# Four low parts of the last token quarter on GpSimd instead of VectorE, and their high parts earlier on ScalarE

## The chip, the cores and the metric

The program runs on one core of a Trainium2 chip. The metric is the device time in microseconds (us) of one execution; the median of three runs of the kernel before is 2413.59 us (2409.25 to 2414.49).

## The reference

A backbone of two layers on 1024 latent tokens and 256 context tokens, width 1024. Layer 0: a combined projection, neighbourhood attention and a bidirectional recurrence, an output projection. Layer 1: a gated short convolution. Each layer ends in a SwiGLU feed-forward block of hidden width 2816. What the change touches is the first projection of three blocks:

```
h = h + g2 * swiglu(modulate(rmsnorm(h, norm2_g[l]), sh2, sc2), w_gu, w_down)   # layer 0 and layer 1
bg, cg, xv = split(modulate(rmsnorm(h, norm1_g), sh1, sc1) @ w_in, 3)           # short convolution
```

All arithmetic is float32. Every output of these blocks is a product of the modulated tokens with a 1024-row weight matrix.

## The kernel before, in words

**Split operands.** A float32 operand is written as a high part (rounded by a copy, on ScalarE) and a low part (full minus high). A product is three matmuls per 128 rows of the contraction: L1014 (high weights, high tokens), L1015 (low weights, high tokens) and L1016 (high weights, low tokens).

**Stages.** Three stages use one scheme: F0 (feed-forward of layer 0), S (short convolution) and F1 (feed-forward of layer 1). Each has a joint (normalise the tokens, make the operands), then "pairs" of output tiles (22, 12 and 22), then the down projection. A pair of tiles is computed by a seven-product scheme on halves of the contraction and halves of the tokens: the products 0 to 6 take sums and differences of token quarters and of weight quarters, and VectorE adds the seven results in PSUM. Products 0 and 3 of the first four pairs are done ahead, in the joint, from their own slots. Product 6 takes the token quarter `a22`, which needs no sum. Products 1, 2, 4 and 5 take sums that VectorE makes: sums 1 and 2 go to `low_f`, their high and low parts to `act_lo`; sums 4 and 5 are made in `x_rms`, with high and low parts in `act_hi`. Each operand consists of four blocks of 128x512, k = 0 to 3.

**Order of the joint (all queues are written by hand, each engine runs its own in order).**

- ScalarE (`joint`, L1524): modulates the second half of the tokens, then `token_high` (L1470) for 1, 2, then `operand_high` (L1491, a high part of the weights, tile `slot_hi`) for product 4, `token_high` for 5, `operand_high` for 5, `token_high` for 4, `operand_high` for 6, `token_high` for 6.
- VectorE (`joint`, L1944): `token_sum` 1 and 2, `token_low` 1 (L1937), `token_sum` 5 (L1929) in turns with `token_low` 2, `token_sum` 4 (L1931) in turns with `token_low` 4, `token_low` 5, `pair_first` (L2012, L2014: the first two PSUM additions of pair 0), `token_low` 6. Then `pair_work` of pair 0 (L2027 `t_pad`, the weight sums L1901 and L1906 for pair 1, L2032, L2034 `t_pad`, L1909, and so on).
- GpSimd: the low parts of the weights, `operand_low` (L975, tile `slot_lo`), for products 1, 2, 4, 5, 6 of pair 0, then pair after pair.
- TensorE (`pair_products`, L1331): products 1, 2, 4, 5, 6. Product n waits for its `slot_lo`; in pair 0 each of its four blocks also waits for its token low part (`ready`). Product 1 of the next pair waits for the PSUM sum C22 (L2034), product 6 for U2 (L2014).
- SyncE: `load_pair` (L683) loads two tiles `raw` of weights for the next pair. They wait for `slot_lo` of product 5 and of product 6 of the pair before; the weight sum L1901 of the next pair waits for both tiles.

Of the kernel before, what the change touches and what calls it, by code (L numbers as in the profile page):

```python
# [24 lines left out]
ALU = mybir.AluOpType  # L25
# [33 lines left out]
def backbone(nc, t):  # L59
# [18 lines left out]
    with es:  # L78
        def sem(name):
            return es.enter_context(nc.semaphore(name))  # L80
# [198 lines left out]
        s_down = {"a0": sem("set_a_first_half_landed"), "a1": sem("set_a_second_half_landed"), "b": sem("set_b_landed"), "c": sem("set_c_landed")}  # L279
        s_h2, s_l2 = sem("down_operand_hi"), sem("down_operand_lo")  # L280
        s_n0, s_fs, s_hs, s_ld = sem("first_half_lo"), sem("token_sums_made"), sem("token_operand_hi"), sem("token_operand_lo")
        s_grow = sem("gain_row_landed")
        s_fturn, s_fsq, s_fstd = sem("fin_turned"), sem("fin_squared"), sem("fin_rms_ready")
        s_fta, s_fpart = sem("fin_first_half_turned"), sem("fin_first_half_squared")
# [76 lines left out]
        REST = (1, 2, 4, 5, 6)  # L361
# [109 lines left out]
            return 16 * st + {1: 2 * k + 1, 2: 2 * k + 2, 5: 8 + k + 1, 4: 12 + k + 1}[n]  # L471

        def highs(st, n, k):
            return 20 * st + 4 * (1, 2, 5, 4, 6).index(n) + k + 1

        def weights_in(st):
            return t["o_w_in"][0] if st == S else t["ffn_w_gu"][0 if st == F0 else 1]
# [323 lines left out]
        def _(pool):  # L801
# [190 lines left out]
            for st in (F0, S, F1):  # L992
                if st != F0:
                    first_lows(st)
                for f in range(FT):
                    first_half_low(st, f)
                if st == F0:
                    first_lows(st)
                operand_low(st, *FIRST[7])
                for n in REST:  # L1000
                    operand_low(st, n, 0)
                for p in range(1, PAIRS[st]):
                    for n in operands(st, p):
                        operand_low(st, n, p)
                for r in range(ROUND[st]):
                    down_low(st, r)
# [3 lines left out]
        def _(pe):  # L1010
# [320 lines left out]
            def pair_products(st, p):  # L1331
                g = PAIR0[st] + p
                every = p >= EARLY
                def ready(n):
                    return (lambda k: (s_ld, 20 * st + 4 * REST.index(n) + k + 1)) if p == 0 else None

                if every:
                    pe.wait_ge(s_xfree, g)
                    operand_product(st, 0, p, x_bank(p))
                if g:  # L1340
                    pe.wait_ge(*made(g - 1, C22))
                operand_product(st, 1, p, P5_BANK, ready(1))
                if g:
                    pe.wait_ge(*made(g - 1, C21))
                operand_product(st, 2, p, P6_BANK, ready(2))
                if every:
                    pe.wait_ge(s_p1, g + 1)
                    operand_product(st, 3, p, x_bank(p))
                operand_product(st, 4, p, P7_BANK, ready(4))
                operand_product(st, 5, p, P3_BANK, ready(5))  # L1350
                pe.wait_ge(*made(g, U2))
                operand_product(st, 6, p, P4_BANK, ready(6))
# [83 lines left out]
        def _(act):  # L1436
# [28 lines left out]
            def token_high(st, n, k):  # L1465
                if n == 6:
                    act.wait_ge(s_nhi, 8 * (NORM[st] + 1) + 2 * k + 2)
                else:
                    act.wait_ge(s_fs, summed(st, n, k))
                nc.scalar.copy(ACTS[n][k][HI], LOW_F[n][k]).then_inc(s_hs, 1)  # L1470
# [53 lines left out]
            def joint(st):  # L1524

                n, n0 = NORM[st], LAST_OUT[st]
                if st != F0:
                    for e in range(7):
                        operand_high(st, *FIRST[e])
                for f in range(FT):  # L1530
                    square(n, f, (s_hup, n0 + f + 3))
                rms(n)
                square(n + 1, 0, (s_hup, n0 + FT + 3))
                if st == S:
                    act.wait_ge(s_const, 5)
                for f in range(FT):
                    first_half(st, f)
                    if f % 2:
                        square(n + 1, 1 + f // 2, (s_hup, n0 + FT + 1 + f // 2 + 3))
                if st == F0:  # L1540
                    for e in range(7):
                        operand_high(st, *FIRST[e])
                for f in range(5, FT):
                    square(n + 1, f, (s_hup, n0 + FT + f + 3))
                first_product_copied(st, 0)
                rms(n + 1)
                first_product_copied(st, 1)
                operand_high(st, *FIRST[7])
                operand_high(st, 1, 0)
                second_half(st, 0)  # L1550
                second_half(st, 1)
                token_high(st, 1, 0)
                operand_high(st, 2, 0)
                second_half(st, 2)
                token_high(st, 1, 1)
                first_product_copied(st, 2)
                second_half(st, 3)
                token_high(st, 1, 2)
                token_high(st, 1, 3)
                for k in range(4):  # L1560
                    token_high(st, 2, k)
                    if k == 1:
                        first_product_copied(st, 3)
                operand_high(st, 4, 0)
                for k in range(4):
                    token_high(st, 5, k)
                operand_high(st, 5, 0)
                for k in range(4):
                    token_high(st, 4, k)
                operand_high(st, 6, 0)  # L1570
                for k in range(4):
                    token_high(st, 6, k)

            def pair_work(st, p):
                ahead = p + 1 if p + 1 < PAIRS[st] else None
# [250 lines left out]
        def _(dve):  # L1826
# [117 lines left out]
            def joint(st):  # L1944

                n, n0, gate = NORM[st], LAST_OUT[st], (G1, G2, MODS + G1)[st]
                for f in range(FT):
                    if st == F0 and f in (0, 3, 6):
                        dve.wait_ge(s_reload[f // 3], 16)
                    update(n0, f, gate, last_bank(st, f))  # L1950
                    if st == S:
                        mods_here(ROUND[F0] - 2, f)
                    if f:
                        add_squares(n, f - 1)
                add_squares(n, FT - 1)
                update(n0, FT, gate, last_bank(st, FT))
                if st == S:
                    mods_here(ROUND[F0] - 2, FT)
                    dve.wait_ge(s_mset, LT + MODS)
                    set_gains((3, mods, MODS + SC1, PAR["n1"] + FT), (4, mods, MODS + SC2, PAR["n2"] + FT))  # L1960
                    dve.wait_ge(s_const, 5)
                inverse_rms(n)
                update(n0, FT + 1, gate, last_bank(st, FT + 1))
                scale(n, 0, 0)
                scale(n, 1, 1)
                add_squares(n + 1, 0)
                for f in range(2, FT):
                    if f < 5:
                        update(n0, FT + f, gate, last_bank(st, FT + f))
                        scale(n, 2 * f - 2, 2 * f - 2)  # L1970
                        scale(n, 2 * f - 1, 2 * f - 1)
                    else:
                        update(n0, FT + f, gate, last_bank(st, FT + f))
                    add_squares(n + 1, f - 1)
                add_squares(n + 1, FT - 1)
                weight_sum(st, 1, 0)
                weight_sum(st, 2, 0)
                inverse_rms(n + 1)
                weight_sum(st, 4, 0)
                weight_sum(st, 6, 0)  # L1980
                order = [(i, i // 2 + 4 * (i % 2)) for i in range(8)]
                scale(n + 1, *order[0])
                scale(n + 1, *order[1])
                for k in range(4):
                    if k < 3:
                        scale(n + 1, *order[2 * k + 2])
                    token_sum(st, 1, k)
                    if k < 3:
                        scale(n + 1, *order[2 * k + 3])
                    token_sum(st, 2, k)  # L1990
                for k in range(4):
                    token_low(st, 1, k)
                for k in range(4):
                    token_sum(st, 5, k)
                    token_low(st, 2, k)
                token_sum(st, 4, 0)
                for k in range(4):
                    if k < 3:
                        token_sum(st, 4, k + 1)
                    token_low(st, 4, k)  # L2000
                for k in range(4):
                    token_low(st, 5, k)
                pair_first(st, 0)
                for k in range(4):
                    token_low(st, 6, k)

            def pair_first(st, p):
                g = PAIR0[st] + p
# [359 lines left out]
```

## Time and profile before

| what | us |
|---|---|
| median of three runs | 2413.59 |
| the profiled execution's own time | 2408.06 |
| its span | 2406.2 |
| TensorE matmul busy | 2310.3 (96% of the span) |
| VectorE busy | 1489.1 (62%) |
| GpSimd busy | 1218.6 (51%) |
| ScalarE busy | 844.3 (35%) |

In a timeline each row gives the start, the time taken, the engine, the line, the operation, the tiles (output, arrow, inputs) and a count of merged neighbours; brackets give the idle time of the engine before it and what ended that. The joint of F0 lies at 600 to 667 us of the span, that of S at 1340 to 1407, that of F1 at 1686 to 1753.

### The profile page before, as it was taken

What the parts mean: (1) busy time and instruction counts of PE and PEld (TensorE: products, weight loads), DVE (VectorE), ACT (ScalarE), POOL (GpSimd) and SP (SyncE); (2) the same over time, 40 slices, a digit from 0 to 9 for tenths busy, and PEclk for the clock granted to TensorE, in tenths of its full rate; (3) what the DMA queues carried; (4) which work ended last, traced back from release to release, by engine and by line L of the source; (5) the groups of instructions that cost most, each with busy time, mean ns of one, the idle gap of its engine ahead of it and who ended that gap; (6) DMA issues with size and microseconds to landing.
All of it is one profiled execution on the core that took longest, in us unless ns stands there. A gap on an engine that the chain in (4) does not pass through costs nothing.

```text
span 2406.2 us, 27721 instructions
## 1 busy us (share of the span) xinstructions
PE 2310.3 (96%) x10486; PEld 1866.6 (78%) x10486; DVE 1489.1 (62%) x1951; ACT 844.3 (35%) x1367; POOL 1218.6 (51%) x739
## 2 busy tenths in 40 slices
PE   8999999989999999999898988999999999999998
PEld 3888878878778888877777867887778888888887
DVE  5677748853775455546666797664875445555553
ACT  4544428862532232331111522222632232232122
POOL 3333346888655555564334255555355555565440
PEclk9999999999999999999998999999999999999999
DMA  9444467534123222255454012243023222243222
GB/s 311 157 137 139 156 158 149 97 98 128 48 84 100 80 79 79 79 184 188 157 187 163 23 58 69 77 140 108 14 92 93 87 79 79 79 149 105 92 84 79
DMA packets 265448, 268.65 MB, mean 112 GB/s; under 512 B 43527, under 2 KB 209123, under 8 KB 264803
## 3 DMA queue, kind: packets, MB, share of 16 engines
q1 hardware_dynamic: 258835, 247.99, 33.6%
q10 hardware_dynamic: 5904, 16.78, 2.0%
q8 instruction: 84, 1.38, 0.2%
q0 software_dynamic: 576, 2.10, 0.2%
q14 instruction: 49, 0.40, 0.1%
HBM read 219.28 MB, written 47.55 MB: 111 GB/s over the span
## 4 chain that ended last, share of the span: by engine, by line
PE 78%; DVE 9%; DMA 5%; POOL 3%; ACT 2%; issue 2%; SPq 1%; DVEq 0%; POOLq 0%; ACTq 0%
PE bank L1014 24%; PE bank L1016 24%; PE bank L1015 24%; DMA mod_in_f<-in_mod_w 3%; POOL slot_lo L975 2%; DMA raw<-in_ffn_w_gu 1%; PE bank L1095 1%; DVE probs L2298 1%; PE bank L1225 1%; SPq L740 1%; PE bank L1251 1%; PE bank L1250 1%; DVE act_hi L1937 1%; PE bank L1212 1%; PE bank L1049 1%
## 5 line engine op out<-in xcount | busy, mean ns | idle before, releaser
L975 POOL TENSOR_TENSOR slot_lo<-raw,slot_hi 128x512 fp32r<-128x512 f32 x256 | 414.3, 1643 | 303.1 <-ACT slot_hi L1491 303.1
L1864 DVE SCALAR_TENSOR_TENSOR h<-bank,mods,h 128x512 f32<-128x512 f32 x384 | 284.9, 749 | 268.2 <-PE bank L1016 265.4
L1491 ACT CAST slot_hi<-raw 128x512 fp32r<-128x512 f32 x256 | 153.5, 619 | 361.4 <-DMA raw<-in_ffn_w_gu 234.7
L1014 PE MATMUL bank<-a,slot_hi 128*128 128x512 f32 x672 | 267.1, 398 | 9.8 <-DVE t_pad L2046 6.3
L1016 PE MATMUL bank<-a,slot_hi 128*128 128x512 f32 x672 | 264.6, 394 | 0.0
L1015 PE MATMUL bank<-a,slot_lo 128*128 128x512 f32 x672 | 263.6, 392 | 0.0
L975 POOL TENSOR_TENSOR slot_lo<-t_sum,slot_hi 128x512 fp32r<-128x512 f32 x112 | 168.8, 1528 | 182.2 <-ACT slot_hi L1491 182.2
L2012 DVE TENSOR_TENSOR bank<-bank,p 128x512 f32<-128x512 f32 x56 | 39.0, 697 | 308.5 <-PE bank L1016 308.4
L1014 PE MATMUL bank<-act_lo,slot_hi 128*128 128x512 f32 x448 | 179.6, 401 | 10.0 <-DVE t_pad L2034 8.0
L1014 PE MATMUL bank<-act_hi,slot_hi 128*128 128x512 f32 x448 | 179.1, 400 | 6.8 <-DVE act_hi L1937 6.5
L1016 PE MATMUL bank<-act_hi,slot_hi 128*128 128x512 f32 x448 | 177.7, 397 | 0.0
L1016 PE MATMUL bank<-act_lo,slot_hi 128*128 128x512 f32 x448 | 177.6, 397 | 0.0
L1015 PE MATMUL bank<-act_lo,slot_lo 128*128 128x512 f32 x448 | 177.5, 396 | 0.0
L1015 PE MATMUL bank<-act_hi,slot_lo 128*128 128x512 f32 x448 | 177.3, 396 | 0.0
L1014 PEld LDWEIGHTS bank<-a,slot_hi 128*128 128x128 f32 x672 | 126.6, 188 | 40.9 <-DVE t_pad L2046 6.8
L986 POOL TENSOR_TENSOR act_lo<-low_f,act_lo 128x512 fp32r<-128x512 f32 x80 | 102.0, 1316 | 109.7 <-ACT act_lo L1522 109.7
L1016 PEld LDWEIGHTS bank<-a,slot_hi 128*128 128x128 f32 x672 | 126.6, 188 | 30.4
L1015 PEld LDWEIGHTS bank<-a,slot_lo 128*128 128x128 f32 x672 | 126.8, 189 | 28.8
L1015 PE MATMUL bank<-act_hi,w_lo 128*128 128x512 f32 x376 | 148.0, 394 | 0.0
L1014 PE MATMUL bank<-act_hi,w_hi 128*128 128x512 f32 x368 | 144.8, 393 | 2.7 <-DVE act_lo L2164 2.7
L1491 ACT CAST slot_hi<-t_sum 128x512 fp32r<-128x512 f32 x112 | 69.7, 622 | 219.3 <-DVE t_sum L1901 198.4
L1016 PE MATMUL bank<-act_lo,w_hi 128*128 128x512 f32 x368 | 144.4, 392 | 0.0
(288 smaller groups left out, 5520.8 us busy)
## 6 DMA issues: line engine op xcount, KB each, us to landing
raw<-in_ffn_w_gu SPq DMA_DIRECT2D x88, 512.0 KB, 4.7
mod_in_f<-in_mod_w SPq DMA_DIRECT2D x48, 512.0 KB, 8.3
z_spill<-silu_g SPq DMA_DIRECT2D x88, 256.0 KB, 4.0
mod_in_p<-in_mod_w SPq DMA_DIRECT2D x32, 512.0 KB, 6.5
raw<-in_o_w_in SPq DMA_DIRECT2D x24, 512.0 KB, 4.6
raw<-in_e_w_in SPq DMA_DIRECT2D x20, 512.0 KB, 5.0
low_f<-z_spill SPq DMA_DIRECT2D x40, 256.0 KB, 4.2
a_f<-z_spill SPq DMA_DIRECT2D x18, 512.0 KB, 6.0
```

Of the source, the lines that this page charges most:

```text
L740: sp.dma_start(down_operand(st, r, j, c, h)[2], from_).then_inc(s_down[set_of(st, r) + ("" if h is None else str(h))], 16)
L975: nc.gpsimd.tensor_tensor(slot_lo[:, s, :], from_, slot_hi[:, s, :], ALU.subtract).then_inc(s_wlo, 1)
L986: nc.gpsimd.tensor_tensor(lo, full, hi, ALU.subtract).then_inc(s_l2, 1)
L1014: pe.matmul(dst, w_hi, x_hi, start=first, stop=False)
L1015: pe.matmul(dst, w_lo, x_hi, start=False, stop=False)
L1016: return pe.matmul(dst, w_hi, x_lo, start=False, stop=last)
L1049: mm = pe.matmul(bank[:, b, m:m + 1], acc[:, m * P:(m + 1) * P], ones[:, 0:1], start=True, stop=True)
L1095: mm = pe.matmul(bank[0:2, 4 + 2 * c + a, :], cond[:, k, :], mod_ring[:, u % 8, a * HALF:(a + 1) * HALF], start=(k == 0), stop=(k == FT - 1))
L1212: pe.matmul(out_, q, k_hi[:, hd % 2, src:src + n], start=True, stop=False)
L1491: nc.scalar.copy(slot_hi[:, s, :], from_).then_inc(s_whi, 1)
L1864: V.scalar_tensor_tensor(out=dst, in0=bank[:, b, :], scalar=mods[:, gate, m:m + 1], in1=dst, op0=ALU.mult, op1=ALU.add).then_inc(s_hup, 1)
L2012: V.tensor_tensor(x, x, first, ALU.add).then_inc(s_made, 1)
```

## The change

GpSimd makes the four low parts of product 6's tokens, between `slot_lo` of product 2 and `slot_lo` of product 4. VectorE's four are gone from behind `pair_first`. ScalarE makes the four high parts after those of 2, ahead of `slot_hi` of product 4 and of the high parts of 5 and 4. A new semaphore counts GpSimd's four; the numbering of ScalarE's high parts follows the new order.

```diff
         def highs(st, n, k):
-            return 20 * st + 4 * (1, 2, 5, 4, 6).index(n) + k + 1
+            return 20 * st + 4 * (1, 2, 6, 5, 4).index(n) + k + 1
...
                 operand_low(st, *FIRST[7])
-                for n in REST:
+                operand_low(st, 1, 0)
+                operand_low(st, 2, 0)
+                for k in range(4):
+                    pool.wait_ge(s_hs, highs(st, 6, k))
+                    hi, lo = ACTS[6][k]
+                    nc.gpsimd.tensor_tensor(lo, LOW_F[6][k], hi, ALU.subtract).then_inc(s_lp, 1)
+                for n in (4, 5, 6):
                     operand_low(st, n, 0)
...
                 def ready(n):
-                    return (lambda k: (s_ld, 20 * st + 4 * REST.index(n) + k + 1)) if p == 0 else None
+                    if p:
+                        return None
+                    return lambda k: (s_lp, 4 * st + k + 1) if n == 6 else (s_ld, 16 * st + 4 * REST.index(n) + k + 1)
...
                     if k == 1:
                         first_product_copied(st, 3)
+                for k in range(4):
+                    token_high(st, 6, k)
                 operand_high(st, 4, 0)
...
                 operand_high(st, 6, 0)
-                for k in range(4):
-                    token_high(st, 6, k)
...
                 pair_first(st, 0)
-                for k in range(4):
-                    token_low(st, 6, k)
```

## Rows read from the trace of the kernel before

**Rows 1.** The page, shares of the engines and the chain that ended last.

```profile
PE 2310.3 (96%) x10486; PEld 1866.6 (78%) x10486; DVE 1489.1 (62%) x1951; ACT 844.3 (35%) x1367; POOL 1218.6 (51%) x739
...
PE 78%; DVE 9%; DMA 5%; POOL 3%; ACT 2%; issue 2%; SPq 1%; DVEq 0%; POOLq 0%; ACTq 0%
```

**Rows 2.** TensorE's waits in the whole span: total us, times, longest.

```profile
PE bank L1014 <- DVE t_pad L2034: 8.0, 7, 2.3
...
PE bank L1014 <- DVE a L1937: 1.2, 2, 0.6
```

**Rows 3.** Timeline of TensorE, F0 joint and first pairs, rows with a wait.

```profile
661.88 0.47 PE L1014 MATMUL bank<-a,slot_hi 128*128 128x512 f32 x1 [0.57 <-DVE a L1937]
...
666.94 0.47 PE L1014 MATMUL bank<-act_lo,slot_hi 128*128 128x512 f32 x1 [2.04 <-DVE t_pad L2034]
...
698.02 0.47 PE L1014 MATMUL bank<-act_lo,slot_hi 128*128 128x512 f32 x1 [0.94 <-DVE t_pad L2034]
701.73 0.50 PE L1014 MATMUL bank<-act_lo,slot_hi 128*128 128x512 f32 x1 [0.67 <-DVE p L2052]
714.38 0.50 PE L1014 MATMUL bank<-a,slot_hi 128*128 128x512 f32 x1 [1.18 <-ACT silu_g L1508]
```

**Rows 4.** Timeline of ScalarE, F0 joint.

```profile
643.36 1.14 ACT L1470 CAST act_lo<-low_f 128x512 fp32r<-128x512 f32 x2
644.40 0.62 ACT L1491 CAST slot_hi<-raw 128x512 fp32r<-128x512 f32 x1
...
648.67 0.62 ACT L1470 CAST act_hi<-x_rms 128x512 fp32r<-128x512 f32 x1 [0.58 <-DVE x_rms L1929]
```

**Rows 5.** Timeline of VectorE, F0 joint.

```profile
649.15 1.28 DVE L1931 TENSOR_TENSOR x_rms<-x_rms,a 128x512 f32<-128x512 f32 x2
650.52 1.62 DVE L1937 TENSOR_TENSOR act_hi<-x_rms,act_hi 128x512 fp32r<-128x512 f32 x1
652.07 1.77 DVE L1931 TENSOR_TENSOR x_rms<-x_rms,a 128x512 f32<-128x512 f32 x1
...
661.06 2.48 DVE L1937 TENSOR_TENSOR a<-a_f,a 128x512 fp32r<-128x512 f32 x4
663.47 0.68 DVE L2027 TENSOR_TENSOR t_pad<-bank,p 128x512 f32<-128x512 f32 x1
664.07 0.67 DVE L1901 TENSOR_TENSOR t_sum<-raw 128x512 f32<-128x512 f32 x1
```

**Rows 6.** One line, L975 on GpSimd: count, shortest/median/longest ns, first and last start; the three joints.

```profile
L975 POOL TENSOR_TENSOR slot_lo<-raw,slot_hi x2: 1731/4109/6487, 645.1 to 651.6; 128x512 fp32r<-128x512 f32 x2
...
L975 POOL TENSOR_TENSOR slot_lo<-raw,slot_hi x2: 1725/4107/6489, 1384.6 to 1391.0; 128x512 fp32r<-128x512 f32 x2
...
L975 POOL TENSOR_TENSOR slot_lo<-raw,slot_hi x2: 1732/4117/6502, 1731.5 to 1738.0; 128x512 fp32r<-128x512 f32 x2
```

**Rows 7.** Timeline of GpSimd, F0 joint.

```profile
645.11 8.18 POOL L975 TENSOR_TENSOR slot_lo<-raw,slot_hi 128x512 fp32r<-128x512 f32 x2 [7.74 <-ACT slot_hi L1491]
656.29 1.29 POOL L975 TENSOR_TENSOR slot_lo<-raw,slot_hi 128x512 fp32r<-128x512 f32 x1 [3.00 <-ACT slot_hi L1491]
```

**Rows 8.** Loads of `raw`, 655 to 685 us: landing times, last issue for pair 2, its first use.

```profile
DMA to landing us min/median/max: 3.8/4.0/5.2
...
674.59 0.37 SPq L683 DMA_DIRECT2D raw<-in_ffn_w_gu  x1
...
679.84 0.69 DVE L1901 TENSOR_TENSOR t_sum<-raw 128x512 f32<-128x512 f32 x1 [4.07 <-DMA raw<-in_ffn_w_gu]
```

**Rows 9.** Timelines of VectorE and of TensorE in stage S.

```profile
1403.80 0.68 DVE L1901 TENSOR_TENSOR t_sum<-raw 128x512 f32<-128x512 f32 x1
...
1456.98 0.79 PE L1014 MATMUL bank<-a,slot_hi 128*128 128x512 f32 x1 [6.34 <-DVE t_pad L2046]
```

**Rows 10.** Stretches: us, busy (x count) of PE, PEld, DVE, ACT, POOL, PEclk granted, DMA share, GB/s.

```profile
661.80:664.80 3.00, 2.92 (x12) 2.17 (x12) 2.94 (x5) 0.00 (x0) 0.00 (x0) 1.00 0.00 0
...
1457.00:1462.80 5.80, 5.80 (x14) 4.54 (x15) 5.67 (x5) 0.91 (x2) 4.33 (x3) 0.50 0.31 87
```

More of the change, by code:

```diff
@@ L281, in backbone @@
         s_n0, s_fs, s_hs, s_ld = sem("first_half_lo"), sem("token_sums_made"), sem("token_operand_hi"), sem("token_operand_lo")
+        s_lp = sem("last_token_operand_lo_by_pool")
         s_grow = sem("gain_row_landed")
```

## The prediction

> **What bounds the kernel now.** I read the page's shares first: TensorE is busy 96% and carries 78% of the chain that ended last [rows 1]. Only time in which TensorE stands still, or runs at its lower clock, can be won or lost. The view of waits says who makes it stand: 1.2 us go to the low parts of product 6 (`a`) and 8.0 us to the sum C22 (`t_pad`, L2034), of which F0's joint has 2.04 [rows 2, 3]. The timelines of one joint, F0, give the order; the other two repeat it within a few tenths (their long GpSimd operations last 6489 and 6502 ns against 6487) [rows 6]. I work F0 out in its own times and carry it over.
>
> In F0 product 4 can start at 652.15, when VectorE has its first low part (650.52 + 1.62 = 652.15) [rows 5]. Product 6 starts at 661.88 and product 1 of pair 1 at 666.94 after 2.04 us of idling for C22 [rows 3]. VectorE is behind all three: it works without a pause from 650.52 to C22, and the four low parts to be moved take 661.06 to 663.47, 2.4 us [rows 5].
>
> **What is removed: VectorE.** Taken alone, everything from 663.47 on would come 2.4 us earlier. TensorE could use it: it idles 0.57 + 2.04 = 2.6 us before product 6 and before pair 1 [rows 3]. So the gain on offer is 2.4 us per joint, 7.2 us in all.
>
> **What moves: ScalarE.** The four high parts cost about 0.52 us each (two take 1.14, starts 0.52 apart; 643.36 + 2 x 0.52 = 644.40) and now run from 644.40 to 646.5; `slot_hi` of product 4 ends near 647.1 instead of 645.0 [rows 4]. The high parts of 5 then run behind, but before they had idled 0.58 us for their sum; the fourth still starts at about 648.67 [rows 4]. From there ScalarE is in its old place. Cost 0; if that cover were thin, it is bounded by 2.1 us of work against VectorE's low parts of 5, which come over 6 us later.
>
> **What is added: GpSimd.** Its price is the heart of the matter. `slot_lo` of product 4 is asked for at 645.1, in the middle of a run of VectorE subtractions and additions with both inputs in SBUF, and lasts 6.49 us; alone such an operation takes 1.29 (656.29) [rows 6, 7]. It ends at 651.59, just after VectorE's first pause (649.15 + 1.28 = 650.43 to 650.52). The VectorE operation that starts at 650.52 takes 1.62 us and the next 1.77, where their like take 0.68; GpSimd's second takes 1.73 [rows 5, 6]. So the two don't run side by side: the request that comes into an unbroken run of VectorE waits for a pause (all three joints, [rows 6]), and after that they take turns, GpSimd's ends being 653.29 - 651.59 = 1.70 apart and VectorE losing 1.1 us per turn.
>
> The Trainium skill (SBUF — State Buffer, "Who interferes with whom") says that a VectorE instruction with two SBUF inputs contends with a GpSimd one that reads SBUF, and that whichever issues first gets the shared ports for the whole instruction while the other blocks until it finishes. The trace agrees on the blocking (1.62, 1.77) and not on the wait, which is ten VectorE operations long and not one. By that rule the loss per joint would be 2.3 instead of the 2.9 below.
>
> The first of the four new operations is asked for when ScalarE's first high part of 6 is done, 644.40 + 0.62 = 645.0. That is the same run of VectorE, which the change leaves as it is up to 650.43. So it ends at 651.6, as `slot_lo` of product 4 did, and behind it stand six more in turns of 1.70: the other three end at 653.3, 655.0 and 656.7, `slot_lo` of 4, 5 and 6 at 658.4, 660.1 and 661.8. Before they ended at 651.6, 653.3 and 657.6 [rows 6, 7].
>
> **What is late next.** VectorE waits seven times for about 1.1 us here and had waited three times: low parts of 4 end at 652.15, 655.5, 658.9, 660.6, the first of 5 at 662.3, the last at 664.1 (0.60 apart once GpSimd is through). `pair_first` starts at 664.1 instead of 659.86, its two steps take 1.2, and L2027 starts at 665.3 instead of 663.47: +1.8, although four operations were taken off.
>
> The load of the second `raw` tile for pair 1 is issued at `slot_lo` of product 6, 661.8 instead of 657.6. Loads in this stretch take 3.8 to 5.2 us to land; in pair 2, whose two loads also go out close together, the last is issued at 674.59 and L1901 starts 5.2 us later [rows 8]. Here the two are 1.7 us apart, so I take 5.2: L1901 starts at 667.0 instead of 664.07, +2.9 (with 3.8 it would be +1.5, but then L2027's +1.8 counts). From L1901 to TensorE's restart are 666.94 - 664.07 = 2.9 us as before, hence product 1 of pair 1 at 669.8: **+2.9 us**.
>
> TensorE itself: product 4 waits for `slot_lo` until 658.5, six microseconds of idling that were not there. At the full clock (12 matmuls in 2.8 us, as product 6 of before within its 3.0 us) [rows 10] it ends with its last low part at 661.4, product 5 at 665.2, product 6 at 668.2. After 6.34 us of idling in stage S the granted clock was 0.50, its 1.2 GHz level, for 5.8 us more [rows 9, 10]; with 5.80 / 14 = 0.41 us per matmul for as long, product 6 ends at 669.1. Both are before 669.8, so this stays hidden.
>
> Does the shift last? In pairs 1 to 3 the idling before 698.02 is again for C22, behind an L1901 that waits for its load (4.07 us in pair 2), which waits for `slot_lo` of product 6 [rows 3, 8]. That ring is what got late, so the shift is passed on whole.
>
> In S the same step gives 1401.3 + 5.2 = 1406.5 for L1901, which stood at 1403.8 [rows 9]: +2.6 (its GpSimd operations lie 739.5 us behind those of F0, 1384.6 against 645.1 [rows 6]). F1 is as F0: +2.9. **Sum: 2.9 + 2.6 + 2.9 = 8.4 us.** On the profiled execution's 2408.06 (span 2406.2 plus 1.9 around it) that is 2416.5. This execution lies 5.5 us under the median of the runs shown, so I add the sum to the median: 2413.6 + 8.4 = **2422.0 us**. Bounds from the same rows: +1.8 per joint (5.4, 2419) if the loads come quickly, +4.6 per joint (13.8, 2427.4) in the clock rival below.
>
> **Rivals.**
>
> *Faster: the turns cost VectorE nothing at the wrong place.* If GpSimd's four operations slip in between VectorE's or ScalarE delivers early enough for the 7.74 us in which GpSimd idled before 645.11 [rows 7], the 2.4 us taken off VectorE come through at L2027, product 6 and C22: 3 x 2.4 = 7.2, 2406.4 us. It decides from the point where `slot_lo` of 4 still ends by 653. For it: the real idling behind exactly these operations [rows 2, 3]. Against it: the high parts are ready at 645.0 at the earliest, and three of three requests at this place waited 6.5 us [rows 6]. Chance 0.11.
>
> *No change: the delay is taken up later.* TensorE idles 0.94 + 0.67 + 1.18 = 2.8 us in pairs 3 and 4 of F0 [rows 3] and 6.34 in S [rows 9]. Were these waits for a chain that is not late, 0.1 of F0's 2.9, none of S's 2.6 and, taking F1 as F0, 0.1 there would be left: +0.2, 2413.8 us. Against it stands that the waits end with the same load ring. Chance 0.15.
>
> *GpSimd is let in at once* (the page's order, as a mechanism here: the first new operation runs behind the VectorE operation that is under way at 645.1). Then six turns run from 645.6 to 655.3, the low parts of 2 come out at up to 655.9, those of 4 end near 660.6, `slot_lo` of 6 follows its high part at 662.4, and a lone load (4.0) lets L1901 start at 666.4: +2.3 per joint, 2420.6. VectorE loses the same turns elsewhere. For: the turns of 1.70. Against: rows 6. Chance 0.10.
>
> *The clock decides.* If TensorE stays at 0.50 for some 10 us from 658.5, products 4, 5 and 6 end at 671.5 and not 669.1: +4.6 per joint, 2427.4. For: one stretch of 5.8 us at 0.50 after such an idling [rows 10]; against: it takes nearly twice that in all three. Chance 0.08.
>
> **How the numbers follow.** The forecast, ring and turns with +5.4 to +10 in all, has 0.56. Faster (by over 0.2%, 4.8 us, about what a measurement can tell here) 0.11; within 0.2% 0.15; slower 0.56 + 0.10 + 0.08 = 0.74. The range 2414 to 2428 leaves out the faster case, and a little at the top.
>
> **What would show it.** In each joint: GpSimd's first `a` operation lasts about 6.5 us from 645, then six operations of about 1.73; `slot_lo` of 4 ends near 658.4; TensorE has one idle stretch of about 6 us before product 4; VectorE's operations from 650.5 last 1.7 each, seven in a row; the wait before pair 1 falls from 2.0 to below 1.7, and VectorE's L1901 of pair 1 waits for a DMA. I am wrong if `slot_lo` of 4 ends before 654, or if pair 1 starts less than 1 us later and pairs 3 and 4 show less idling.

## The result and the profile after

The changed kernel takes 2415.4 us (median of 20 runs, 2407.5 to 2423.2), the kernel before in the same jobs 2409.5 us (20 runs, 2403.7 to 2414.5). The ratio is 1.0024 (95% interval 1.0013 to 1.0034): **slower by 5.8 us** (3.1 to 8.2). I had forecast slower by 8.4 us, at 2422.0. The direction came as written, and so did the operations named and their times in F0's joint. The measured size is a third smaller, and the median of three runs on which I put the sum, 2413.6, lies 4.1 us above what 20 runs of the kernel before give.

The profile page of the changed kernel, shares of the engines (compare [rows 1]): GpSimd has the four operations of three joints more, VectorE fewer operations and yet more busy time.

```profile
PE 2313.2 (96%) x10486; PEld 1872.5 (78%) x10486; DVE 1492.2 (62%) x1939; ACT 842.7 (35%) x1367; POOL 1239.3 (51%) x751
```

The view of one line after, the new low parts on GpSimd (L1006) in the joints of F0 and S: count, shortest/median/longest ns, first and last start (compare [rows 6]).

```profile
L1006 POOL TENSOR_TENSOR a<-a_f,a x4: 1710/1714/6508, 644.7 to 654.5; 128x512 fp32r<-128x512 f32 x4
...
L1006 POOL TENSOR_TENSOR a<-a_f,a x4: 1702/1711/6502, 1387.1 to 1396.9; 128x512 fp32r<-128x512 f32 x4
```

The timeline of GpSimd after, F0 joint (compare [rows 7]): four low parts to 656.25, then the weights of 4, 5 and 6 to 661.31.

```profile
644.73 11.52 POOL L1006 TENSOR_TENSOR a<-a_f,a 128x512 fp32r<-128x512 f32 x4 [7.74 <-ACT a L1479]
656.22 5.09 POOL L976 TENSOR_TENSOR slot_lo<-raw,slot_hi 128x512 fp32r<-128x512 f32 x3
```

The timeline of VectorE after, same stretch (compare [rows 5]). The row of 6.94 us stands for six operations, of which the first three last 1.75 to 1.77.

```profile
650.16 1.63 DVE L1946 TENSOR_TENSOR act_hi<-x_rms,act_hi 128x512 fp32r<-128x512 f32 x1
651.72 1.74 DVE L1940 TENSOR_TENSOR x_rms<-x_rms,a 128x512 f32<-128x512 f32 x1
653.38 1.75 DVE L1946 TENSOR_TENSOR act_hi<-x_rms,act_hi 128x512 fp32r<-128x512 f32 x1
655.06 1.74 DVE L1940 TENSOR_TENSOR x_rms<-x_rms,a 128x512 f32<-128x512 f32 x1
656.73 6.94 DVE L1946 TENSOR_TENSOR act_hi<-x_rms,act_hi 128x512 fp32r<-128x512 f32 x6
...
664.90 0.69 DVE L2034 TENSOR_TENSOR t_pad<-bank,p 128x512 f32<-128x512 f32 x1
666.42 0.69 DVE L1910 TENSOR_TENSOR t_sum<-raw 128x512 f32<-128x512 f32 x1 [0.83 <-DMA raw<-in_ffn_w_gu]
...
669.15 0.68 DVE L1918 TENSOR_TENSOR raw<-raw 128x512 f32<-128x512 f32 x1
```

TensorE after, rows of the timeline with a wait (compare [rows 3]), then two stretches (columns as in [rows 10]). One idling of 6.19 us ahead of product 4 takes the place of the small ones; behind it the granted clock is 0.50 for 5.7 us.

```profile
657.98 0.79 PE L1021 MATMUL bank<-act_hi,slot_hi 128*128 128x512 f32 x1 [6.19 <-POOL slot_lo L976]
684.21 0.47 PE L1021 MATMUL bank<-act_lo,slot_hi 128*128 128x512 f32 x1 [0.55 <-DVE t_pad L2041]
699.41 0.47 PE L1021 MATMUL bank<-act_lo,slot_hi 128*128 128x512 f32 x1 [0.88 <-DVE t_pad L2041]
```

```profile
657.90:663.60 5.70, 5.62 (x13) 4.45 (x14) 5.70 (x7) 0.07 (x1) 3.41 (x3) 0.50 0.42 113
663.60:669.00 5.40, 5.40 (x24) 4.12 (x22) 4.40 (x8) 1.60 (x3) 1.10 (x1) 0.99 0.26 78
```

**Where the time lies.** I follow one marker, the first weight sum of every pair (L1901 before, L1910 after), and take the shift between the two profiles. "Kept" is what a joint and its first pairs have added from pair 6 on; from there the shift stays constant to the end of the stage.

| stretch | at pair 1 | kept |
|---|---|---|
| F0 joint | +2.7 | +1.8 |
| F0 down projection | | +1.2 |
| S joint | +1.7 | +0.6 |
| S down projection | | +2.0 |
| F1 joint | +2.5 | +1.7 |

The three joints keep 4.1 us. With -0.4 us that lay ahead of the F0 joint this makes the profiles' 6.9 us (2413.1 against 2406.2); 3.2 of them fall in two down projections, which the change doesn't touch. The rows of stretches (columns as in [rows 10]) show what most of S's 2.0 us is: ahead of the joint of F1 the kernel before has 3.4 us at a granted clock of 0.50, the changed kernel 6.8.

```profile
1664.30:1667.70 3.40, 3.40 (x9) 2.63 (x9) 0.75 (x1) 0.63 (x1) 3.40 (x4) 0.50 0.02 5
```

```profile
1667.20:1674.00 6.80, 5.93 (x14) 4.73 (x15) 0.75 (x1) 0.63 (x1) 6.80 (x6) 0.50 0.01 2
```

In the stretches behind these, at 1.00, a matmul takes 0.22 us (33 in 7.30 us, 27 in 6.00), so 9 of them in 3.40 us lost 1.4 and 14 in 5.93 lost 2.9: an estimate of 1.4 us more, of the 2.0. Why the stretch is longer, these rows don't say.

### The profile page after: what moved, and what is told of

Read it like the earlier page. It is cut to its first block, busy times and chain, and to the rows that moved or that the text cites. A ratio compares the mean times of both kernels' runs of the same rounds, so it can differ in the third digit from the quotient of the medians.

```text
span 2413.1 us, 27721 instructions
## 1 busy us (share of the span) xinstructions
PE 2313.2 (96%) x10486; PEld 1872.5 (78%) x10486; DVE 1492.2 (62%) x1939; ACT 842.7 (35%) x1367; POOL 1239.3 (51%) x751
## 4 chain that ended last, share of the span: by engine, by line
PE 78%; DVE 6%; DMA 6%; POOL 5%; ACT 2%; issue 2%; SPq 1%; DVEq 0%; POOLq 0%; ACTq 0%
PE bank L1021 24%; PE bank L1023 24%; PE bank L1022 24%; DMA mod_in_f<-in_mod_w 3%; POOL slot_lo L976 2%; DMA raw<-in_ffn_w_gu 2%; POOL a L1006 1%; PE bank L1102 1%; DVE probs L2305 1%; PE bank L1232 1%; SPq L741 1%; PE bank L1258 1%; PE bank L1257 1%; PE bank L1219 1%; PE bank L1056 1%
## 5 line engine op out<-in xcount | busy, mean ns | idle before, releaser
L976 POOL TENSOR_TENSOR slot_lo<-raw,slot_hi 128x512 fp32r<-128x512 f32 x256 | 399.8, 1586 | 267.3 <-ACT slot_hi L1500 267.1
```

What stands on the lines that cost most here:

```text
L976: nc.gpsimd.tensor_tensor(slot_lo[:, s, :], from_, slot_hi[:, s, :], ALU.subtract).then_inc(s_wlo, 1)
```

## The experiments

All were timed in five rounds beside the kernel before; differences are the ratio's distance from 1 times 2410 us, in brackets their interval. Times of a joint are given relative to that joint's start where two kernels are compared.

**The changed kernel again.** No edit.

> The changed kernel once more, for a second profile of it. Theory (turns): in each joint GpSimd's seven operations run in turns with VectorE, slot_lo of 4 ends 6.3 us later than before, and the shift left after pair 4 is about 1.8 us in F0, 0.9 in S and 1.7 in F1, 4.4 in all, in this profile too; what the down projections added between the two profiles (1.1 in F0's, 2.0 in S's) comes out otherwise, since nothing of them was changed. In all 1.0024 again, 3 to 8 us over the kernel before. Rival (down phases): the later start of the down projections costs time by itself, and 1.1 and 2.0 us are found again in the same places.

Ratio 1.0016 (1.0004 to 1.0028), +3.9 us (1.0 to 6.7). GpSimd's turns are there again; the joints keep +1.9, +0.5 and +2.3, 4.8 in all. The down projections add 1.5 and 1.6 us, near the 1.2 and 2.0 of the first profile. I had expected them to come out otherwise; it is the rival's sign that was met.

Over all twelve profiles F0's down projection is shifted against the kernel before by -1.8 to +8.9 us, also where a kernel is faster. The three largest shifts (+5.7, +7.1, +8.9) stand in the three profiles with 10.2 us at 0.50 from 1161 or 1162 us on. S's is shifted by +1.6 to +2.0 in four profiles (the changed kernel twice, the low parts last, the low parts between `slot_lo` of 5 and of 6), which all have 6.8 us at 0.50 ahead of F1, and by -1.5 to +1.1 in the other eight, which have 3.4 us or none. So the shift in S goes with the length of that stretch. The low parts last have it too and show no loss. Whether the change brings the longer stretch about stays open.

**ScalarE's order alone.**

```diff
 # kernel before
+                for k in range(4):
+                    token_high(st, 6, k)
                 operand_high(st, 4, 0)
...
                 operand_high(st, 6, 0)
-                for k in range(4):
-                    token_high(st, 6, k)
```

> The kernel before with ScalarE's new order alone: the high parts of 6 ahead of slot_hi of 4 and of the high parts of 5 and 4; VectorE makes the low parts of 6 where it did. Theory (turns): no change, 0 us (-1 to +1): slot_lo of 4 is asked for 2.1 us later, in the same unbroken run of VectorE, and ends at 651.6 as before. Rival (ScalarE's order is what costs): the high parts of 5 and 4 and slot_hi come 2.1 us late and are waited for, up to +2.1 us per joint, +2 to +6 in all.

Ratio 0.9998 (0.9985 to 1.0011), -0.5 us (-3.6 to +2.7). No cost of ScalarE's part can be seen, as the prediction had it. One thing showed by the way: in F0 the weight sum of pair 1 comes at the same time as in the kernel before, and yet this profile is 1.3 us ahead from pair 6 on. The clock isn't the reason, both have 3.4 us at 0.50 in pair 1 (first the kernel before, then this one):

```profile
667.60:671.00 3.40, 3.40 (x10) 2.63 (x9) 3.30 (x5) 2.07 (x4) 2.06 (x2) 0.50 0.04 14
```

```profile
668.10:671.50 3.40, 3.40 (x10) 2.63 (x9) 3.30 (x5) 2.07 (x4) 2.07 (x3) 0.50 0.12 44
```

So what one joint keeps can differ by 1.3 us between two profiles with the same joint; in S and F1 it is +0.2 and +0.4 here.

**Low parts last.**

```diff
 # changed kernel, GpSimd
-                operand_low(st, 1, 0)
-                operand_low(st, 2, 0)
-                (the four low parts of 6)
-                for n in (4, 5, 6):
+                for n in REST:
                     operand_low(st, n, 0)
+                (the four low parts of 6)
```

> The changed kernel, but GpSimd makes the four low parts of 6 behind slot_lo of 6 instead of ahead of slot_lo of 4. Theory (turns, and the loads behind slot_lo): slot_lo of 4, 5 and 6 end where they did in the kernel before (651.6, 653.3, 657.6), the loads are not late, L1901 of pair 1 does not wait for a DMA; two of the four operations meet VectorE's last low parts of 5 (1.1 us each), the others its PSUM additions, which they don't disturb. VectorE is then 0.2 to 1.3 us earlier than before per joint: -0.5 to -4 us against the kernel before, 6 to 9 under the changed kernel. Rival (GpSimd can't do this work for VectorE at any place, each operation costs VectorE 1.1 us and frees 0.6): +2 us per joint, as the changed kernel.

Ratio 0.9994 (0.998 to 1.0008), -1.4 us against the kernel before (-4.8 to +1.9). The loss is gone, a gain isn't shown. The timeline of GpSimd in this kernel says why there is none:

```profile
646.78 6.11 POOL L976 TENSOR_TENSOR slot_lo<-raw,slot_hi 128x512 fp32r<-128x512 f32 x2 [9.82 <-ACT slot_hi L1498]
655.89 1.29 POOL L976 TENSOR_TENSOR slot_lo<-raw,slot_hi 128x512 fp32r<-128x512 f32 x1 [3.00 <-ACT slot_hi L1498]
657.15 6.79 POOL L1006 TENSOR_TENSOR a<-a_f,a 128x512 fp32r<-128x512 f32 x4
```

All four took 1.7 us. They drew out three of VectorE's low parts of 5 (1.76 us each), where I had expected two; the PSUM addition beside the fourth took 0.69. Three turns of 1.06 against the 2.4 us freed leave VectorE 0.8 us later, and its weight sum of pair 1 comes 0.9 to 1.0 us late in each joint. `slot_lo` of product 4, asked for 2.1 us later than in the kernel before relative to VectorE's run, still ended at its pause.

**High and low parts early.**

```diff
 # changed kernel, ScalarE
                 second_half(st, 0)
+                token_high(st, 6, 0)
                 second_half(st, 1)
                 token_high(st, 1, 0)
                 operand_high(st, 2, 0)
+                token_high(st, 6, 1)
 # and so on; GpSimd makes each low part at once, behind token_sum 1 of its k
```

> The changed kernel, but ScalarE makes each high part of 6 just behind the second half it is taken from (around 633 to 641 us in F0) and GpSimd its low part at once, in the 7.7 us in which it idled. Theory (turns): part of the four operations fall beside VectorE's multiplications with one input in PSUM, which they don't hold up; the rest costs 1.1 us each. VectorE's run up to low part 4 of k=0 is 1 to 3 us late, and 2.4 us are saved behind it: between -1.4 and +0.6 us per joint, -4 to +2 in all against the kernel before. slot_lo of 4 still takes over 5 us. Rival (any four more operations on GpSimd cost 4 x 0.5 us net): +2 us per joint, +6 in all.

Ratio 0.9996 (0.9981 to 1.001), -1.0 us (-4.6 to +2.4): no change, inside the forecast. One expectation missed: `slot_lo` of 4 did not take over 5 us but 1.53, 1.54 and 1.54 in the three joints, although it was asked for in the middle of VectorE operations with two SBUF inputs and without a pause. GpSimd's row, then VectorE's:

```profile
647.83 1.53 POOL L976 TENSOR_TENSOR slot_lo<-raw,slot_hi 128x512 fp32r<-128x512 f32 x1 [1.97 <-ACT slot_hi L1506]
```

```profile
644.66 3.56 DVE L1954 TENSOR_TENSOR act_lo<-low_f,act_lo 128x512 fp32r<-128x512 f32 x4
648.14 1.77 DVE L1946 TENSOR_TENSOR x_rms<-x_rms,low_f 128x512 f32<-128x512 f32 x1
```

It waited for the one operation under way and held up the next. The changed kernel's loss depends on where GpSimd is asked, not on the four operations being GpSimd's.

**Low parts between `slot_lo` of 5 and of 6.**

```diff
 # changed kernel, GpSimd
-                operand_low(st, 1, 0)
-                operand_low(st, 2, 0)
+                for n in (1, 2, 4, 5):
+                    operand_low(st, n, 0)
                 (the four low parts of 6)
-                for n in (4, 5, 6):
-                    operand_low(st, n, 0)
+                operand_low(st, 6, 0)
```

> The changed kernel, but GpSimd makes the four low parts of 6 between slot_lo of 5 and slot_lo of 6. Product 4 and 5 then get their weights as in the kernel before (651.6, 653.3), while the turns are as many as in the changed kernel and slot_lo of 6 still ends near 661.8, so the loads of pair 1 are as late. Theory (the ring of loads behind slot_lo of 6): L1901 of pair 1 waits for a DMA until about 666.8 (+2.3 to +2.7) and each joint costs as in the changed kernel, +4 to +6 us in all over the kernel before. Rival (the 6.2 us in which TensorE stands still ahead of product 4, and the lower clock after them, are what costs): that idling is gone, so is the loss, -1 to +1 us in all.

Ratio 1.0016 (1.0006 to 1.0026), +3.9 us (1.4 to 6.3), as much as the changed kernel in its second timing: product 4's wait for its weights isn't needed for the loss. TensorE has two idlings instead, both for VectorE's low parts, and around them 6.8 us at 0.50, as long as in the changed kernel (from 659.4 on):

```profile
657.23 0.50 PE L1020 MATMUL bank<-act_hi,slot_hi 128*128 128x512 f32 x1 [2.33 <-DVE act_hi L1945]
660.59 0.79 PE L1020 MATMUL bank<-act_hi,slot_hi 128*128 128x512 f32 x1 [2.40 <-DVE act_hi L1945]
```

Since the lower clock came here as well, this run doesn't take it away; what it can have cost is bounded in the section on the prediction.

One part of the expectation missed. VectorE's weight sum of pair 1 did not wait for a DMA here; it followed the PSUM addition directly:

```profile
666.94 0.69 DVE L2033 TENSOR_TENSOR t_pad<-bank,p 128x512 f32<-128x512 f32 x1
667.63 0.69 DVE L1909 TENSOR_TENSOR t_sum<-raw 128x512 f32<-128x512 f32 x1
```

In the changed kernel the load was the later by 0.83 us in F0 and 0.59 in F1, and in S there was no wait for it. So VectorE's own lateness and the late load lie close together, and the runs don't separate them.

**No low parts of 6 on any engine** (product 6 takes the high part twice; this part of the computation is left out).

```diff
 # changed kernel
-                (the four low parts of 6)
...
-                    mm = product(bank[:, bank_, :], w, *ACTS[n][k], k == 0, k == 3)
+                    hi, lo = ACTS[n][k]
+                    mm = product(bank[:, bank_, :], w, hi, hi if n == 6 else lo, k == 0, k == 3)
 # and ready(6) waits for the high parts instead
```

> The changed kernel without the four low parts of 6 on any engine: product 6 takes the high part in place of the low one in L1016 (this part of the computation is left out). It shows what VectorE's relief is worth when GpSimd is asked for nothing. Theory (turns): VectorE has 2.4 us less and loses no turn more than before, L2027 and L1901 of pair 1 come 2.4 us earlier (L1901 at 661.7, where its load lands), -2 us per joint, -4 to -7 in all against the kernel before. Rival (the idling before pair 1 has another cause): -1 to +1.

Ratio 0.9953 (0.9936 to 0.9969), -11.3 us (-15.4 to -7.5), more than expected. L1901 of pair 1 comes 2.3, 2.4 and 2.3 us earlier in the three joints, 7.0 us as in the sum; from pair 6 on the joints keep 4.3, 3.2 and 2.7, 10.2 in all. 2.8 of the additional 3.2 us arise between the weight sums of pair 1 and pair 2. There VectorE's sum `raw<-raw` takes 0.68 us in all three joints, where it took 1.8 in the kernel before; the section on the prediction comes back to it.

**Half the width** (the same part is left out, GpSimd runs four subtractions of 128x256).

```diff
 # kernel without low parts, GpSimd where the changed kernel has its four
+    nc.gpsimd.tensor_tensor(lo[:, 0:256], LOW_F[6][k][:, 0:256], hi[:, 0:256], ALU.subtract)
```

> As the kernel without low parts (product 6 takes the high part twice, that part of the computation is left out), but GpSimd runs four subtractions of half the width, 128x256, where the changed kernel has its four. Theory (turns): each holds VectorE up for about 0.55 instead of 1.1 us and GpSimd's next operation likewise; slot_lo of 6 ends near 659.6 (661.3 in the changed kernel, 657.6 before), L1901 of pair 1 starts 0.3 to 1 us later than before; 0 to +3 us in all. Rival (a fixed cost per GpSimd operation): as the changed kernel, +4 to +6.

Ratio 0.9997 (0.9983 to 1.0011), -0.7 us (-4.1 to +2.7), just below the forecast of 0 to +3, with an interval that covers most of it. The timeline of VectorE shows the size of a turn:

```profile
649.11 1.06 DVE L1947 TENSOR_TENSOR act_hi<-x_rms,act_hi 128x512 fp32r<-128x512 f32 x1
650.10 1.22 DVE L1941 TENSOR_TENSOR x_rms<-x_rms,a 128x512 f32<-128x512 f32 x1
651.24 1.21 DVE L1947 TENSOR_TENSOR act_hi<-x_rms,act_hi 128x512 fp32r<-128x512 f32 x1
652.37 1.21 DVE L1941 TENSOR_TENSOR x_rms<-x_rms,a 128x512 f32<-128x512 f32 x1
```

1.21 us instead of 1.74 in the changed kernel, 0.68 without GpSimd: the loss is 0.53 for half the width and 1.06 for the whole. It goes with the length of GpSimd's operation and has no fixed part that can be seen. L1901 of pair 1 is 0.6 us late in F0, as expected (0.3 to 1), but only 0.25 in F1 and 0.4 early in S.

**Weights of product 4 early.**

```diff
 # kernel before, ScalarE
                 first_product_copied(st, 2)
+                operand_high(st, 4, 0)
                 second_half(st, 3)
...
-                operand_high(st, 4, 0)
                 for k in range(4):
                     token_high(st, 5, k)
```

> The kernel before with one operation moved: ScalarE makes slot_hi of product 4 ahead of the last second half (near 638.5, when its slot has come free), so that GpSimd makes slot_lo of 4 in its idle time, beside VectorE's multiplications with an input in PSUM. Theory (turns): GpSimd has one operation less in VectorE's unbroken run, slot_lo of 5 takes its place in the wait until 651.6, and VectorE loses one turn of 1.1 us less between 650.5 and the sum C22: 0 to -1.1 us per joint, -3.3 to +0.5 in all. Rival (VectorE's turns are not what bounds the joint): 0.

Ratio 0.9985 (0.9971 to 0.9999), -3.6 us (-7.0 to -0.2), just past the -3.3 expected. L1901 of pair 1 comes 0.8 us earlier in each joint. The same operation that took 6.49 us takes 1.29, here in GpSimd's timeline:

```profile
640.22 1.29 POOL L975 TENSOR_TENSOR slot_lo<-raw,slot_hi 128x512 fp32r<-128x512 f32 x1 [1.72 <-ACT slot_hi L1491]
651.26 1.71 POOL L975 TENSOR_TENSOR slot_lo<-raw,slot_hi 128x512 fp32r<-128x512 f32 x1 [9.76 <-ACT slot_hi L1491]
656.58 1.30 POOL L975 TENSOR_TENSOR slot_lo<-raw,slot_hi 128x512 fp32r<-128x512 f32 x1 [3.61 <-ACT slot_hi L1491]
```

**The reverse of the change.**

```diff
 # kernel with the weights of product 4 early
-                for n in REST:                 # GpSimd
+                for n in (1, 2, 4):
                     operand_low(st, n, 0)
...
+            def weight_low(st, n):             # VectorE
+                at_ = product_at(st, n, 0)
+                dve.wait_ge(s_wlo, at_)
+                dve.wait_ge(s_whi, at_ + 1)
+                V.tensor_tensor(slot_lo[:, n, :], raw[:, 0 if n == 6 else 1, HALF:], slot_hi[:, n, :], ALU.subtract).then_inc(s_wlo, 1)
 # weight_low 5 behind token_low(st, 4, 1), weight_low 6 behind token_low(st, 5, 1)
```

> The reverse of the change. On top of the kernel with slot_hi and slot_lo of product 4 made early, VectorE makes slot_lo of 5 and of 6 of pair 0 itself (behind low part 4 of k=1 and low part 5 of k=1), and its four low parts of 6 stay where they were. GpSimd is asked for nothing in VectorE's run. Theory (turns: a GpSimd operation in that run costs VectorE 1.1 us, the same operation on VectorE 0.6): VectorE loses three turns less (3.2 us) and does two operations more (1.2 us), -2 us per joint, and slot_lo of 6, and with it the loads of pair 1, comes 1 to 2 us earlier; product 4 meets no wait. L1901 of pair 1 at 661 to 662 in F0 (664.07 before), -2 to -3 us per joint, -6 to -10 in all. Rival (VectorE is the full engine here and every operation added to it costs): +1.2 us per joint, +3.6 in all.

Ratio 0.9971 (0.9959 to 0.9984), **-7.0 us** (-9.9 to -3.9), with two operations more on VectorE in each joint. Its run there has no drawn-out operation left:

```profile
652.53 0.68 DVE L1937 TENSOR_TENSOR act_hi<-x_rms,act_hi 128x512 fp32r<-128x512 f32 x1
653.13 0.68 DVE L1943 TENSOR_TENSOR slot_lo<-raw,slot_hi 128x512 fp32r<-128x512 f32 x1
653.73 0.69 DVE L1931 TENSOR_TENSOR x_rms<-x_rms,a 128x512 f32<-128x512 f32 x1
654.34 2.66 DVE L1937 TENSOR_TENSOR act_hi<-x_rms,act_hi 128x512 fp32r<-128x512 f32 x4
```

This kernel beats the kernel before and the changed one. L1901 of pair 1 is 1.7 us earlier in each joint (2 to 3 expected in F0), where the early weights of 4 alone gave 0.8, and the joints keep 2.3, 2.1 and 1.3 us. Against the kernel with the early weights alone the times are not clearly apart (-7.0 against -3.6 us, intervals overlap); it is the place of L1901 that shows what the two weights on VectorE add.

**The reverse, and the low parts of 6 on GpSimd beside PSUM additions.**

```diff
 # kernel before this one, GpSimd behind operand_low of 1, 2 and 4
+                pool.wait_ge(s_ld, 16 * st + 16)
+                (the four low parts of 6, none on VectorE)
```

> As the kernel before this one, and GpSimd makes the four low parts of 6 only after VectorE's last low part of 5, beside VectorE's PSUM additions, which a GpSimd operation doesn't hold up. Theory: VectorE has another 2.4 us less, but L1901 of pair 1 then waits for its load, so little more comes of it than in the kernel with the two weights on VectorE: 0 to -1 us per joint against that one, -6 to -12 in all against the kernel before. Rival (GpSimd's 4 x 1.3 us make product 6 late): the last low part near 662, product 6 ends at most 1 us later than in the other; 0 to +1 us per joint against it.

Ratio 0.9968 (0.9955 to 0.9981), -7.7 us (-10.8 to -4.6). The four take 5.45 us together, 1.36 each, and no PSUM addition is drawn out; the weight sum behind them, with both inputs in SBUF, is (1.79). The two kernels can't be told apart (their intervals nearly coincide): product 6 now waits for GpSimd, and VectorE, 2.4 us freer, for its load.

```profile
657.96 5.45 POOL L1007 TENSOR_TENSOR a<-a_f,a 128x512 fp32r<-128x512 f32 x4 [17.96 <-DVE act_hi L1945]
```

```profile
657.79 0.69 DVE L2028 TENSOR_TENSOR bank<-bank,p 128x512 f32<-128x512 f32 x1
658.39 0.68 DVE L2030 TENSOR_TENSOR p<-bank,p 128x512 f32<-128x512 f32 x1
659.11 0.69 DVE L2043 TENSOR_TENSOR t_pad<-bank,p 128x512 f32<-128x512 f32 x1
660.48 1.79 DVE L1909 TENSOR_TENSOR t_sum<-raw 128x512 f32<-128x512 f32 x1 [0.68 <-DMA raw<-in_ffn_w_gu]
```

**Low parts last and weights of 4 early.** Both edits above together.

> The changed kernel with its four GpSimd operations behind slot_lo of 6, and slot_hi and slot_lo of product 4 made early. Theory: the two shifts add, one turn less in VectorE's run: -1 us per joint against the kernel with the low parts last, -2 to -5 in all against the kernel before. Rival (the early weights only helped by luck): as the kernel with the low parts last, -1.4.

Ratio 0.9989 (0.9977 to 1.0001), -2.7 us (-5.5 to +0.2): as expected, but not clear of no change.

## Why the prediction was right in kind and wrong in size

- **ScalarE's move costs nothing:** right, as far as the run with its order alone can tell (-0.5 us, -3.6 to +2.7).
- **The first request waits for VectorE's pause, the others take turns:** right at this place (6.51 us, then 1.71 each; `slot_lo` of 4 and of 6 end at 657.93 and 661.31, 658.4 and 661.8 forecast for a joint that starts 0.4 later). Half the width halved the turn. As a rule for every unbroken run it is wrong. `slot_lo` of 4 in the kernel with everything early got in after one VectorE operation, and so did `slot_lo` of 6 in the kernel before: asked for at 656.29 inside a VectorE operation, it took 1.29 us while the VectorE operation of 656.33 took 1.80. The prediction read this row as an operation "alone", which it was not. 1.29 us beside an operation with an input in PSUM (0.74 us, not drawn out) is shown by the early weights of 4. The wait at 645.11 is nine VectorE operations long, not ten.
- **L2027 +1.8, L1901 +2.9, a wait for a DMA there:** +1.8 (664.90 with the joint 0.4 earlier), +2.7, and a wait of 0.83. Right for F0; F1 gave 2.5 instead of 2.9, and S 1.7 instead of 2.6. This is the first mis-sized term: the three sum to 6.9, not 8.4. For S I had taken the landing time from F0, but there the load was in time and VectorE's own +1.7 decided.
- **TensorE's idling and lower clock stay hidden:** the idling (6.19) and the stretch at 0.50 came. In F0 product 6 ends at 669.2 and C22 at 669.24, so they are level; in F1 product 6 ends 0.3 us behind C22. All three joints have 6.8 us at 0.50, where the kernel before has 3.4, none and 3.4. But product 1 of pair 1 starts 2.92, 2.92 and 2.97 us behind the weight sum, against 2.87 or 2.88 before, and at most 3.10 in the kernel with the low parts between `slot_lo` of 5 and of 6. So up to there the lower clock cost at most 0.1 us a joint here and 0.2 there, and the clock is back at 1.00. With the wait for `slot_lo` of 4 taken away the loss stayed (+3.9 us).
- **"The shift is passed on whole": this step failed.** Of the 6.9 us at pair 1, 4.1 are left from pair 6 on. 2.5 of these 2.8 us go between the weight sums of pair 1 and pair 2 (0.90, 0.75 and 0.85 in the three joints). In the kernel before, GpSimd's second operation of pair 1 starts 0.03 us ahead of VectorE's L1909, which then takes 1.81, 1.80 and 1.80 us. VectorE's row and GpSimd's, before:

```profile
666.78 1.81 DVE L1909 TENSOR_TENSOR raw<-raw 128x512 f32<-128x512 f32 x1
```

```profile
665.53 2.52 POOL L975 TENSOR_TENSOR slot_lo<-t_sum,slot_hi 128x512 fp32r<-128x512 f32 x2 [7.95 <-ACT slot_hi L1491]
```

  In the changed kernel the two start level, the same sum (L1918) goes first and takes 0.68 us in all three joints, and GpSimd waits instead (3.09 for 2.52 us):

```profile
667.90 3.09 POOL L976 TENSOR_TENSOR slot_lo<-t_sum,slot_hi 128x512 fp32r<-128x512 f32 x2 [6.59 <-ACT slot_hi L1500]
```

  I had counted the turns in the joint and not those in the pairs behind it. All profiles taken together bear it out: in S the stretch from pair 1 to pair 2 is 14.4 us in the six profiles where this sum takes 0.68, and 15.2 in the six where it takes 1.8 (the kernel with the low parts beside PSUM additions is apart, 16.3). No run moves this one order by itself. A few hundredths of a microsecond decide it, and in F0 the two profiles of the changed kernel differ in it (0.68 and 1.84), so that it fell the costly way in all joints before and the cheap way in all joints after is in part luck.
- **The down projections: a term put at nothing.** They show +3.2 us in the first profile and +3.1 in the second. Whether that belongs to the change stays open, so how the measured 5.8 and 3.9 us divide between joints and the rest does too.
- **The base:** a median of three that was 4.1 us high. It moved the forecast time by more than the sum was off (8.4 forecast, 5.8 measured).
- The page's order as a rival (GpSimd let in at once, from the Trainium skill, SBUF — State Buffer, "Who interferes with whom") did not occur at the place where it was forecast: GpSimd's first operation lasted 6.5 us in the joints after the change as well. It did occur for the two `slot_lo` named above. The rule's other half, that the engine that is second blocks, agrees with VectorE's 0.53 us of loss for half the width and 1.06 for the whole.

## What to carry to other kernels

Price an operation that is moved from VectorE to GpSimd by what it does to VectorE's queue: here it freed 0.60 us and cost 1.06 us when it met operations with two SBUF inputs, and the move in the other direction, with one request moved into GpSimd's idle time, won 7 us. Look for where GpSimd's request falls: beside operations with an input in PSUM it cost VectorE nothing. A delay found at one place is not the delay at the end: +6.9 us at pair 1 became +4.1 here, and -7.0 without the low parts became -10.2. Follow a marker through the profile before taking a shift over whole.

## What the runs showed of the hardware

- At one place of the joint a GpSimd subtraction that asks in the middle of an unbroken run of VectorE operations with two SBUF inputs waits for the first pause, 0.08 us long: 6.5 us, in three of three joints. Asked for 2.1 us later in the same run it ends at the same moment (4.4 us). At two other places it got in after the one operation under way (1.29 and 1.53 us in all). What decides between the two, no run here shows.
- Once both have something waiting they alternate strictly, 0.6 us VectorE, 1.1 us GpSimd. The waiting stood in the trace of before; that the alternation holds over seven operations without a slip was an assumption.
- Where both engines are ready within 0.03 us of each other, either can be let in first. It costs VectorE 1.1 us (1.81 for 0.68) or GpSimd 0.55 us (1.84 for 1.29).
- Profiles of kernels that differ only in the joints differ by up to 10.7 us in F0's down projection (-1.8 to +8.9), and the three largest shifts stand beside a stretch of 10.2 us at 0.50 that the others lack there. The kernel before alone took 2399.0 to 2416.3 us in 35 executions.
